# Seven block products for the output projection of one more token tile, with the summed weights made in DRAM

## The chip, the cores and the metric

One Trainium2 chip, one core. The time is the device time of one execution in microseconds; the figure shown for a kernel is the median of its runs.

## The reference

One hybrid encoder block over 2048 tokens of width 1024, in float32. Cut to what matters:

```python
h = rmsnorm(x, w_norm_pre)
q_a, k_a, v_a, z_a, q_r, f_r, i_r, z_r = split(h @ w_in)      # 3328 columns
o_a = sliding_window_sink_attention(rope(q_a), rope(k_a), v_a, sinks) * silu(z_a)
o_r = rmsnorm(hgrn2_chunkwise(q_r, f_r, i_r, lb), hgrn_norm) * silu(z_r)
y = concatenate([o_a, o_r]) @ w_out                            # (2048, 1024) @ (1024, 1024)
out = x + rmsnorm(y, w_norm_post)
```

## The kernel before

The tokens go in four tiles of 512 (TILES, t = 0 to 3). In each tile the tensor engine (PE) first forms 26 column blocks of the input projection (w = 0 to 25: key, value, four queries, four gates, then for each of four recurrent heads forget gate, query, value, gate), 24 matmuls of 128x512 each: eight blocks of the inner dimension, times three for a float32 product made of halves (high x high, low x high, high x low; `products`). Then comes the output projection. Attention and the recurrence of the same tile run between these matmuls, at places that `between` gives (w, m: weight tile and matmul within it): scores of pair q at w = SCORES0 + 2q (8, 10, 12, 14), m = 4; the turn of the previous pair's probabilities right behind; the weighing of the values (`weigh`) at m = 20 of the same weight tile.

Tiles 0 and 1 (t < FAST = 2) use `out_plain`: 8 blocks k x 4 token blocks x 2 column halves x 3 = 192 matmuls of 128x512. Tiles 2 and 3 use `out_fast`, a seven-product scheme after Strassen and Winograd on 2 x 2 blocks: UNITS lists 56 products of three matmuls, 168 in all, over 14 weight tiles (FAST_ROWS). Eight of these (T1 to T4, two weight tiles each, T_TILES = 8) are sums of quarters of the output weights; the sums of the activations are made on the vector engine (DVE) in `sum_head`.

Each weight tile (128x1024, 512 KB) is needed as a rounded high part and a low remainder. For i < FRESH = 40 (i counts weight tiles over all token tiles: all 34 of tile 0 and the first six of tile 1) SP loads the raw weights (`load_raw`, L450) into four slots; the scalar engine (ACT) rounds (`split_hi`, L926) some three steps before use, DVE subtracts (`split_lo`, L1261), and SP saves both parts to DRAM (`save_split`, L458; rows `kept`). A rounding into one of the four split slots waits for the save of the tile that was there (`wait_saved`). From i = 40 on SP loads both parts back (`load_split`, L469).

The summed weights of `out_fast` are made by DVE (`sum_weights`): SP loads four quarters, DVE makes four sums (L1458), ACT rounds (`sums_high`, L1012), DVE subtracts (L1463), SP saves. Half of it happens at the end of tile 1, the other half in steps 5 to 8 of tile 2 (SUMS_AT = 5).

Every engine's order is written by hand, as a loop over t and steps s; step s runs beside weight tile w = s or so, and an engine works strictly in order. In ACT's step: the swap for the rope of the block before (L1066, s - 1 in ROPE_TILES = 0, 2, 3, 4, 5), then gates (`gate_first` L930 to L932, `gate_second` L941, from s = 7), sums_high, splits, softmax (`exp_scores`), `place_values`, and the placement of the values of attention (L1154, s = 2 to 5). In DVE's step: the rope turn (`rope_turn`, L1323 to L1330, s - 2 in ROPE_TILES, so the last in s = 7), gate scaling (L1337), softmax_first, gate_first, sum_weights, splits. PE's first scores wait for the last rope turn (`roped`). GpSimd does small float32 work only; its first wait in tile 0 that is not set-up is in step 18 (L1713, L1697). SP runs a few weight tiles ahead of PE.

The entry: the first two column blocks of tile 0 (K_TILE, V_TILE) follow the order ENTRY, blocks k = 0 to 3 of the first, then of the second, then pairs, as x and weights arrive in parts; FILL puts extra small matmuls in (L877). The sum over x squared (`sum_x`, L589) stands in weight tile 2 at m = 16.

## Time and profile before

| | |
|---|---|
| median of 3 runs | 865.8 us (865.51 to 867.25) |
| the profiled execution | 867.9 us, its span 866.1 us, granted clock 0.997 |
| PE | 853.7 us busy, 99% of the span, 4430 matmuls |
| DVE | 631.8 us, 73% |
| ACT | 518.7 us, 60% |
| GpSimd | 114.6 us, 13% |
| DMA | 211.20 MB, mean 244 GB/s; queue q1 64.5% of 16 engines |

A busy PE counts from the start of a matmul to its modelled end; matmuls overlap (0.39 us each at a start every 0.23), so the starts in the timeline tell more than the busy time.

### The profile page before, as it was taken

To read this page: it belongs to the slowest core of one execution; us is meant where nothing else is said; L and a number is where in the kernel's file an instruction comes from. 1 tells how busy PE (TensorE), PEld (TensorE's weight loads), DVE (VectorE), ACT (ScalarE), POOL (GpSimd) and SP (SyncE) were. 2 spreads that over 40 slices of the span, in tenths; PEclk is the share of its full clock that TensorE was granted. 3 is DMA by queue.
4 is the path that set the end of the run, shared out by engine and by line. 5 is a ranking of instruction groups with operands and counts; after the bars stand their busy time and mean duration, and the time that the engine had idled before them with its cause. 6 is when DMAs were issued, how large, how long until landed. Compare 5 with 4: busy or idle time off the path is not lost.

```text
span 866.1 us, 12450 instructions
## 1 busy us (share of the span) xinstructions
PE 853.7 (99%) x4430; PEld 701.8 (81%) x4430; DVE 631.8 (73%) x1125; ACT 518.7 (60%) x1033; POOL 114.6 (13%) x84
## 2 busy tenths in 40 slices
PE   7999999999999999999999999999999999999997
PEld 6887788888888778888888877888888887888885
DVE  5768878684556799767846789887775368888846
ACT  6756556664556558577436655866753755576544
POOL 0000003521200000433020000144300000004220
PEclk9999999999999999999999999999999999999999
DMA  8587554847987636553899794445699674434586
GB/s 314 182 329 250 219 208 160 314 146 277 418 336 258 228 136 255 182 185 137 312 386 365 257 351 158 159 146 217 226 375 390 236 281 146 146 147 152 193 323 254
DMA packets 59981, 211.20 MB, mean 244 GB/s; under 512 B 6672, under 2 KB 6928, under 8 KB 59920
## 3 DMA queue, kind: packets, MB, share of 16 engines
q1 hardware_dynamic: 57904, 205.56, 64.5%
q10 hardware_dynamic: 2016, 4.85, 1.4%
q8 instruction: 35, 0.57, 0.3%
q14 instruction: 26, 0.21, 0.1%
HBM read 157.95 MB, written 52.43 MB: 243 GB/s over the span
## 4 chain that ended last, share of the span: by engine, by line
PE 80%; DVE 11%; ACT 5%; issue 3%; DMA 1%; SPq 0%; DVEq 0%
PE bank L596 52%; PE bank L605 5%; PE turn_b L852 3%; PE score_b L852 3%; PE bank L852 3%; PE turn_b L605 3%; PE score_b L605 3%; DVE kv_tok L1383 2%; PE turn_b L653 2%; PE score_b L629 2%; PE turn_b L706 1%; PE bank L687 1%; PE turn_b L709 1%; PE bank L697 1%; ACT probs_t L953 1%
## 5 line engine op out<-in xcount | busy, mean ns | idle before, releaser
L596 PE MATMUL bank<-h_hi,w_lo 128*128 128x512 f32 x832 | 327.9, 394 | 0.0
L596 PE MATMUL bank<-h_hi,w_hi 128*128 128x512 f32 x832 | 325.1, 392 | 2.1 <-ACT h_hi L980 2.1
L596 PE MATMUL bank<-h_lo,w_hi 128*128 128x512 f32 x832 | 326.5, 392 | 0.0
L596 PEld LDWEIGHTS bank<-h_hi,w_hi 128*128 128x128 f32 x832 | 156.8, 188 | 34.8 <-ACT h_hi L980 2.6
L596 PEld LDWEIGHTS bank<-h_lo,w_hi 128*128 128x128 f32 x832 | 156.7, 188 | 34.8 <-issue 3.3
L596 PEld LDWEIGHTS bank<-h_hi,w_lo 128*128 128x128 f32 x832 | 156.6, 188 | 33.3 <-issue 0.2
L1713 POOL TENSOR_TENSOR mix_lo<-v_r,mix_hi 128x512 fp32r<-128x512 f32 x16 | 21.2, 1324 | 542.3 <-ACT v_r L1140 542.3
L1261 DVE TENSOR_TENSOR w_lo<-w_raw,w_hi 128x1024 fp32r<-128x1024 f32 x37 | 45.9, 1247 | 35.9 <-ACT w_hi L926 35.4
L1383 DVE STREAM_TRANSPOSE kv_tok<-k_mid 32x128 f32<-32x128 f32 x192 | 58.1, 303 | 2.8
L926 ACT ACTIVATE w_hi<-w_raw 128x1024 fp32r<-128x1024 f32 x38 | 39.7, 1050 | 25.0 <-issue 10.2
L1697 POOL TENSOR_TENSOR x_acc<-x_acc,x_sq 128x512 f32<-128x512 f32 x21 | 32.7, 1559 | 70.0 <-ACT x_sq L976 70.0
L930 ACT ACTIVATE g_a<-g_b 128x512 f32<-128x512 f32 x30 | 18.9, 630 | 38.2 <-DVE g_b L1337 38.2
L941 ACT ACTIVATE g_a<-g_a 128x512 f32<-128x512 f32 x32 | 20.2, 632 | 34.3 <-DVE g_a L1341 34.3
L1066 ACT ACTIVATE f_b<-bank 32x512 f32<-32x512 f32 x48 | 28.3, 589 | 16.5 <-PE bank L596 10.6
L962 ACT ACTIVATE kv_tok<-f_d 32x128 f32<-32x128 f32 x96 | 29.5, 307 | 10.0 <-DVE f_d L1577 9.0
L1341 DVE SCALAR_TENSOR_TENSOR g_a<-g_b,g_a 128x512 f32<-128x512 f32 x30 | 21.6, 722 | 18.3 <-ACT g_a L932 18.3
L962 ACT ACTIVATE probs<-f_d 32x128 f32<-32x128 f32 x96 | 29.5, 307 | 1.2
L1634 DVE TENSOR_TENSOR_SCAN f_c<-reset,f_b 128x512 f32<-128x512 f32 x16 | 19.6, 1224 | 11.3 <-ACT f_b L1123 11.3
L1251 DVE SCALAR_TENSOR_TENSOR h_lo<-x_in,vec,h_hi 128x512 fp32r<-128x512 f32 x32 | 23.3, 773 | 4.8 <-ACT h_hi L980 4.7
L1476 DVE SCALAR_TENSOR_TENSOR q_gate<-q_gate,y_stats,x_in 128x512 f32<-128x512 f32 x28 | 23.1, 873 | 4.5 <-DMA x_in<-in_x_rows 3.6
L605 PE MATMUL bank<-w_hi,mix_lo 128*128 128x512 f32 x64 | 25.3, 395 | 0.0
L605 PE MATMUL bank<-w_hi,mix_hi 128*128 128x512 f32 x64 | 24.9, 390 | 0.0
(280 smaller groups left out, 1549.8 us busy)
## 6 DMA issues: line engine op xcount, KB each, us to landing
w_hi<-kept_hi SPq DMA_DIRECT2D x108, 512.0 KB, 3.7
w_lo<-kept_lo SPq DMA_DIRECT2D x108, 512.0 KB, 4.8
w_raw<-in_weights SPq DMA_DIRECT2D x46, 512.0 KB, 5.9
kept_hi<-w_hi SPq DMA_DIRECT2D x34, 512.0 KB, 6.2
kept_lo<-w_lo SPq DMA_DIRECT2D x34, 512.0 KB, 7.1
x_in<-in_x_rows SPq DMA_DIRECT2D x8, 1024.0 KB, 8.0
x_in<-in_x SPq DMA_DIRECT2D x15, 512.0 KB, 6.7
kept_lo<-w_raw SPq DMA_DIRECT2D x8, 512.0 KB, 6.9
```

What stands on the lines that cost most here:

```text
L596: mm = pe.matmul(acc(w)[:, :], stationary[:, s, k, :], moving[:, k, :], start=(m == 0), stop=(m == 3 * KT - 1), skip_group_check=True)
L605: mm = pe.matmul(y_bank[half][b][:, :], mix[:, k, b * P:(b + 1) * P], weight[:, SPLIT_SLOT[index(t, w)], (k % 2) * 4:(k % 2) * 4 + 4, :].r ...
L852: mm = pe.matmul(into, mix, weight, start=w in (P1A, P7A, P2A, P4A) and k == 0 and part == 0, stop=k == KT // 2 - 1 and part == 2, skip_gr ...
L926: act.activation(w_hi[:, SPLIT_SLOT[i], :, :], w_raw[:, i % RAW_SLOTS, :, :], ACT.Copy).then_inc(hi_split.sem, 1)
L962: copy = act.activation(square(v_tok(t, h), j, i), square(f_d[:, :], i, j), ACT.Copy)
L1066: copy = act.activation(dst[32 * b:32 * b + 32, :], acc(s - 1)[32 * (b ^ 1):32 * (b ^ 1) + 32, :], ACT.Copy)
L1251: dve.scalar_tensor_tensor(h_lo[:, k, :], x_in[:, k, :], w_pre[:, k:k + 1], h_hi[:, k, :], ALU.mult, ALU.subtract).then_inc(h_lo_done.sem, 1)
L1261: dve.tensor_tensor(w_lo[:, s, :, :], w_raw[:, i % RAW_SLOTS, :, :], w_hi[:, s, :, :], ALU.subtract).then_inc(lo_split.sem, 1)
L1341: dve.scalar_tensor_tensor(g_a[:, :], g_b[:, :], 0.0, gate_log(t, i), ALU.min, ALU.subtract).then_inc(gate_arg.sem, 1)
L1383: last = dve.transpose(square(kv_tok[:, 0, :], j, i), square(k_mid[:, :], i, j))
L1476: dve.scalar_tensor_tensor(y, y, y_scale[:, b:b + 1], x_in[:, 2 * b + half, :], ALU.mult, ALU.add).then_inc(finished.sem, 1)
L1697: pool.tensor_tensor(x_acc[:, :], x_acc[:, :], x_sq[:, :], ALU.add).then_inc(x_added.sem, 1)
```

## The change

FAST goes from 2 to 1: tile 1 too uses `out_fast`. The summed weights are no longer made by DVE but in a DRAM tensor `t_rows`: GpSimd issues, in tile 0 as soon as remainder 6 is made, two copies of 1 MB, two accumulating DMAs, then copy, accumulation, copy, accumulation, each waiting for the one before; T1 = B11 + B12, T3 = B22 + B12, T2 = T3 + B11, T4 = T2 + B21. The signs differ from before, so `sum_head` and `post` change signs. SP loads the eight sums (512 KB each): 0 and 1 at (0, OUT0), 2 and 3 at (1, 0), 4 to 7 at (1, 7) of its order; ACT rounds and DVE subtracts them in steps 3 (two), 4 (two), 5 (two), 6 and 7 (one each) of tile 1; SP saves them between its weight tiles 8 and 17. Buffers are those of the probabilities, a spare of the raw area, the raw slots, and the mix tiles.

The entry goes by blocks of two, V's first half is loaded ahead of x's second pair, the vector load stands behind x's first block, a fourth weight tile is split before the loop, the two loads of `squares` move behind ACT's squares of x and their wait from `sum_x` and DVE to the turn of the values; `sum_x` stands at m = 20 in tile 0; one filler fewer.

```diff
+LATE = 6
...
-FAST = 2
+FAST = 1
...
-SPLIT_SLOT += [w % 4 for w in range(WT)] + [(WT + w) % 4 for w in range(FAST_WT)] * (TILES - FAST)
...
+SPLIT_SLOT += [w % 4 for w in range(FAST_WT)] * (TILES - FAST)
...
-SUMS_IN = (FAST - 1, H0 + 8), (FAST, 5)
-SUMS_OUT = ((FAST, 0, 0), (FAST, 1, 2)), ((FAST, H0, 0), (FAST, H0 + 2, 2))
-SUMS_AT = 5
+SUMS_IN = {(FAST - 1, OUT0): (0, 1), (FAST, 0): (2, 3), (FAST, LATE + 1): (4, 5, 6, 7)}
+SUMS_SPLIT = {3: (0, 1), 4: (2, 3), 5: (4, 5), 6: (6,), 7: (7,)}
+SUMS_OUT = {8: 2, 9: 3, 11: 0, 12: 1, 13: 4, 14: 5, 15: 6, 17: 7}
...
-DVE_LOW = range(3, FRESH)
+DVE_LOW = range(4, FRESH)
...
-ENTRY = [(w, k - lag, part) for first, last in ((0, 4), (4, 6), (6, 8)) for w in (K_TILE, V_TILE)
+ENTRY = [(w, k - lag, part) for first, last in ((0, 2), (2, 4), (4, 6), (6, 8)) for w in (K_TILE, V_TILE)
...
-FILL = {1: 1, 2: 2}
+FILL = {1: 1, 2: 1}
...
-        t_hi = [t_more[:, 0, :, :], t_probs[:, 1, :, :], t_more[:, 1, :, :], t_probs[:, 0, :, :]], \
-               [mix[:, 2 * i:2 * i + 2, :] for mix in (mix_hi, mix_lo) for i in range(2)]
+        t_in = [area[:, i, :, :] for area, n in ((t_more, 2), (t_probs, 2), (w_raw, RAW_SLOTS)) for i in range(n)]
+        t_hi = [mix[:, 2 * i:2 * i + 2, :] for i in (2, 3, 1, 0) for mix in (mix_hi, mix_lo)]
...
-                    sp.wait_ge(t_saved, 16 * 2 * T_TILES)
+                    sp.wait_ge(t_saved, 32 * (T_TILES - 2))
+                    sp.wait_ge(probs_saved, 64)
                 for part, rows in ((w_hi, kept[0]), (w_lo, kept[1])):
                     sp.dma_start(part[:, slot, :, :].bitcast(FP32),
                                  rows[row * P:(row + 1) * P, :].rearrange("p (k m) -> p k m", k=KT)).then_inc(w_ready[slot], 16)
 
-            def load_sums(j):
-
-                if j == 0:
-                    sp.wait_ge(lo_split.sem, lo_split.after(0, 0) + FRESH - 1)
-                else:
-                    sp.wait_ge(t_saved, 16 * T_TILES)
-                for r, w in enumerate((B11, B21, B12, B22)):
-                    sp.dma_start(w_raw[:, r, :, :], weights[(w + j) * P:(w + j + 1) * P, :].rearrange("p (k m) -> p k m", k=KT)).then_inc(t_raw, 16)
-
-            def save_sums(j, first):
-
-                sp.wait_ge(t_high, 4 * j + first + 2)
-                sp.wait_ge(t_low, 4 * j + first + 2)
-                for r, w in ((0, T1), (2, T3)) if first == 0 else ((3, T2), (1, T4)):
-                    rows = slice((w + j) * P, (w + j + 1) * P)
-                    sp.dma_start(kept[0][rows, :].rearrange("p (k m) -> p k m", k=2), t_hi[j][r].bitcast(FP32)).then_inc(t_saved, 16)
-                    sp.dma_start(kept[1][rows, :].rearrange("p (k m) -> p k m", k=KT), w_raw[:, r, :, :]).then_inc(t_saved, 16)
+            def load_sum(k):
+
+                if k == 0:
+                    sp.wait_ge(t_made, 64)
+                if k == 2:
+                    sp.wait_ge(weighed.sem, weighed.after(FAST - 1, PAIRS - 1))
+                    sp.wait_ge(head_mixed.sem, head_mixed.after(FAST - 1, HEADS - 1))
+                if k >= 4:
+                    sp.wait_ge(lo_split.sem, lo_split.after(0, 0) + FRESH - RAW_SLOTS + k - 4)
+                sp.dma_start(t_in[k], t_rows[k * P:(k + 1) * P, :].rearrange("p (k m) -> p k m", k=KT)).then_inc(t_loaded[k], 16)
+
+            def save_sum(k):
+
+                sp.wait_ge(t_low, k + 1)
+                rows, saved = slice((WT + k) * P, (WT + k + 1) * P), probs_saved if k in (2, 3) else t_saved
+                sp.dma_start(kept[0][rows, :].rearrange("p (k m) -> p k m", k=2), t_hi[k].bitcast(FP32)).then_inc(saved, 16)
+                sp.dma_start(kept[1][rows, :].rearrange("p (k m) -> p k m", k=KT), t_in[k]).then_inc(saved, 16)
 
...
-            sp.dma_start(vec[:, :], vectors).then_inc(vec_loaded, 16)
...
             sp.dma_start(x_in[:, 0, :], x[0:P, 0:N]).then_inc(x_head, 16)
+            sp.dma_start(vec[:, :], vectors).then_inc(vec_loaded, 16)
             load_half(K_TILE, 0)
             sp.dma_start(x_in[:, 1, :], x[0:P, N:2 * N]).then_inc(x_quarter[0], 16)
+            load_half(V_TILE, 0)
             load_first_x(2)
-            load_half(V_TILE, 0)
             load_half(K_TILE, 1)
             load_first_x(4)
             load_half(V_TILE, 1)
...
+                    for k in SUMS_IN.get((t, w), ()):
+                        load_sum(k)
                     if i >= FRESH:
                         load_split(t, w)
+                    if t == FAST and w in SUMS_OUT:
+                        save_sum(SUMS_OUT[w])
...
-                if w == XSUM and m == (0 if t else 16):
-                    pe.wait_ge(stored[1], 32)
+                if w == XSUM and m == (0 if t else 20):
                     sum_x(t)
                 if w == V_TURN and m == 4 and t < DVE_TURN:
+                    pe.wait_ge(stored[1], 32)
                     turn_values(t)
                 if m == 4 and not odd:
...
-            for i in range(2):
-                act.dma_start(sq_in[:, i, :], squares[:, i * P:(i + 1) * P]).then_inc(stored[1], 16)
...
-            def sums_high(k):
-
-                act.wait_ge(t_sum, k + 1)
-                if k == 4:
-                    act.wait_ge(t_saved, 16 * T_TILES)
-                r = (0, 2, 3, 1)[k % 4]
-                act.activation(t_hi[k // 4][r], w_raw[:, r, :, :].rearrange("p k m -> p (k m)").rearrange("p (k n) -> p k n", k=2), ACT.Copy).then_inc(t_high, 1)
+            def sum_high(k):
+
+                act.wait_ge(t_loaded[k], 16)
+                act.activation(t_hi[k], t_in[k].rearrange("p k m -> p (k m)").rearrange("p (k n) -> p k n", k=2), ACT.Copy).then_inc(t_high, 1)
 
...
             for k in range(1, KT):
                 act.wait_ge(x_quarter[k // 2], 16)
                 round_h(0, k)
+                if k == 1:
+                    first_hi(V_TILE, 0)
                 if k == 3:
-                    first_hi(V_TILE, 0)
                     first_hi(K_TILE, 1)
                 if k == 5:
                     first_hi(V_TILE, 1)
-            split_hi(2)
+            for i in (2, 3):
+                split_hi(i)
             for k in range(KT):
                 act.activation(q_gate[:, k, :], x_in[:, k, :], ACT.Square).then_inc(x_squared.sem, 1)
+            for i in range(2):
+                act.dma_start(sq_in[:, i, :], squares[:, i * P:(i + 1) * P]).then_inc(stored[1], 16)
...
                             act.wait_ge(head_mixed.sem, head_mixed.after(t, head))
+                            if t == FAST and head == 0:
+                                act.wait_ge(t_saved, 32 * (T_TILES - 2))
...
-                    if t == FAST and s in (SUMS_AT + 1, SUMS_AT + 2):
-                        for k in range(2):
-                            sums_high(4 + 2 * (s - SUMS_AT - 1) + k)
+                    for k in SUMS_SPLIT.get(s, ()) if t == FAST else ():
+                        sum_high(k)
...
                             act.wait_ge(o_done.sem, o_done.after(t, head))
+                            if t == FAST and head == 0:
+                                act.wait_ge(probs_saved, 64)
                             act.activation(o_sq_hi, out_b, ACT.Square)
...
-                        for k in range(4) if t == FAST - 1 else ():
-                            sums_high(k)
...
                 dve.wait_ge(s_low.sem, s_low.after(t, h - 1))
-                dve.tensor_tensor(s_tmp[:, S2, :], h_mix[:, 2 * P:], s3[:, h, :], ALU.subtract).then_inc(s_step, 1)
-                dve.tensor_tensor(s_tmp[:, S1, :], h_mix[:, 2 * P:], a21[:, h, :], ALU.add)
+                dve.scalar_tensor_tensor(s_tmp[:, S2, :], h_mix[:, 2 * P:], -1.0, s3[:, h, :], ALU.mult, ALU.subtract).then_inc(s_step, 1)
+                dve.tensor_tensor(s_tmp[:, S1, :], h_mix[:, 2 * P:], a21[:, h, :], ALU.subtract)
                 dve.wait_ge(s_step, (t - FAST) * HEADS + h + 1)
-                dve.tensor_tensor(s_tmp[:, S4, :], h_mix[:, 0:2 * P], s_tmp[:, S2, :], ALU.subtract).then_inc(s_made.sem, 1)
-
-            def sum_weights(j, part):
-
-                raw = lambda r: w_raw[:, r, :, :]
-                if part < 2:
-                    dve.wait_ge(t_raw, 64 * (j + 1))
-                    for k, dst, a, b in ((0, 0, 2, 0), (1, 2, 3, 2)) if part == 0 else ((2, 3, 3, 0), (3, 1, 1, 3)):
-                        if k:
-                            dve.wait_ge(t_sum, 4 * j + k)
-                        dve.tensor_tensor(raw(dst), raw(a), raw(b), ALU.subtract).then_inc(t_sum, 1)
+                dve.scalar_tensor_tensor(s_tmp[:, S4, :], h_mix[:, 0:2 * P], -1.0, s_tmp[:, S2, :], ALU.mult, ALU.subtract).then_inc(s_made.sem, 1)
+
+            def sum_low(k):
+
+                dve.wait_ge(t_high, k + 1)
+                dve.tensor_tensor(t_in[k], t_in[k], t_hi[k].rearrange("p k n -> p (k n)").rearrange("p (k m) -> p k m", m=P), ALU.subtract).then_inc(t_low, 1)
...
-                    if t == FAST and 0 <= s - SUMS_AT < 4:
-                        sum_weights(1, s - SUMS_AT)
+                    for k in SUMS_SPLIT.get(s, ()) if t == FAST else ():
+                        sum_low(k)
...
-            pool.wait_ge(lo_split.sem, lo_split.after(0, 2))
+            pool.wait_ge(lo_split.sem, lo_split.after(0, 6))
+
+            def sum_start(dst, src):
+                pool.dma_start(t_rows[dst * 2 * P:(dst + 1) * 2 * P, :], src).then_inc(t_base, 16)
+
+            def sum_add(dst, src):
+                pool.dma_start(t_rows[dst * 2 * P:(dst + 1) * 2 * P, :], src, accum_op=ALU.add, max_dma_last_dim=4 * KT * P).then_inc(t_made, 16)
+
+            def block_rows(w):
+                return weights[w * P:(w + 2) * P, :]
+
+            sum_start(0, block_rows(B11))
+            sum_start(1, block_rows(B22))
+            pool.wait_ge(t_base, 32)
+            sum_add(0, block_rows(B12))
+            sum_add(1, block_rows(B12))
+            pool.wait_ge(t_made, 32)
+            sum_start(2, t_rows[2 * P:4 * P, :])
+            pool.wait_ge(t_base, 48)
+            sum_add(2, block_rows(B11))
+            pool.wait_ge(t_made, 48)
+            sum_start(3, t_rows[4 * P:6 * P, :])
+            pool.wait_ge(t_base, 64)
+            sum_add(3, block_rows(B21))
...
+    t_rows = nc.dram_tensor("t_rows", (T_TILES * P, KT * P), FP32, kind="Internal").ap()
```

## Rows read from the trace of the kernel before

**Rows 1.** Stretches: us; busy of PE, PEld, DVE, ACT, POOL; clock; DMA share; GB/s

```profile
229.40:442.95 213.55, 213.55 (x1100) 176.11 (x1099) 159.35 (x288) 132.39 (x284) 33.23 (x24) 1.00 0.65 239
...
442.95:652.30 209.35, 208.82 (x1075) 171.43 (x1074) 161.79 (x301) 130.71 (x277) 33.44 (x22) 1.00 0.70 261
```

**Rows 2.** Timeline of PE, end of tile 0: start us, us, what

```profile
229.17 0.39 PE L605 MATMUL bank<-w_lo,mix_hi 128*128 128x512 f32 x1
229.40 0.39 PE L596 MATMUL bank<-h_hi,w_hi 128*128 128x512 f32 x1
```

**Rows 3.** Timeline of PE, tile 2, state products; in brackets idle time and releaser

```profile
588.42 1.13 PE L697 MATMUL bank<-kv_tok 128*128 128x128 f32 x8 [0.22 <-DVE a_t L1355]
```

**Rows 4.** Instructions on w_raw in tile 2, durations ns min/median/max, first and last start

```profile
L1012 ACT ACTIVATE mix_hi<-w_raw x2: 1043/1053/1063, 478.9 to 486.8; 128x1024 fp32r<-128x1024 f32 x2
...
L1463 DVE TENSOR_TENSOR w_raw<-w_raw,mix_hi x2: 1219/1219/1219, 486.7 to 495.4; 128x1024 f32<-128x1024 f32 x2
```

**Rows 5.** Timeline of tile 2, fourth gate on DVE and first weighing on PE

```profile
502.23 0.69 DVE L1337 TENSOR_TENSOR g_b<-bank,x_scale 128x512 f32<-128x512 f32 x1
...
506.02 1.08 PE L653 MATMUL turn_b<-probs_t,v_win 128*64 128x256 f32 x8
```

**Rows 6.** Timeline of ACT, steps 3 to 7 of tile 1; step 5 of tile 2

```profile
254.19 2.39 ACT L1066 ACTIVATE f_d<-bank 32x512 f32<-32x512 f32 x4
...
265.31 2.39 ACT L1066 ACTIVATE f_b<-bank 32x512 f32<-32x512 f32 x4
...
270.38 0.63 ACT L930 ACTIVATE g_a<-g_b 128x512 f32<-128x512 f32 x1 [1.49 <-DVE g_b L1337]
...
471.03 2.39 ACT L1066 ACTIVATE f_d<-bank 32x512 f32<-32x512 f32 x4 [1.46 <-PE bank L596]
```

**Rows 7.** Timeline of DVE, end of the last rope turn in tile 1

```profile
269.06 0.69 DVE L1330 TENSOR_TENSOR q_gate<-f_a,f_b 128x512 f32<-128x512 f32 x1
```

**Rows 8.** Timeline of PE, first scores and first weighing of tile 1

```profile
274.37 1.16 PE L629 MATMUL score_b<-k_t,q_gate 64*128 64x128 f32 x16
...
292.02 1.08 PE L653 MATMUL turn_b<-probs_t,v_win 128*64 128x256 f32 x8
```

**Rows 9.** Busy time by stretch, columns as in rows 1

```profile
35.00:130.00 95.00, 95.00 (x570) 76.08 (x569) 72.85 (x112) 55.35 (x85) 0.06 (x1) 1.00 0.72 257
...
206.00:245.00 39.00, 39.00 (x173) 32.30 (x173) 20.41 (x24) 16.53 (x35) 5.75 (x4) 1.00 1.02 414
```

**Rows 10.** Timeline of ACT and DVE, late weight splits around the start of tile 1

```profile
228.32 1.06 ACT L926 ACTIVATE w_hi<-w_raw 128x1024 fp32r<-128x1024 f32 x1 [2.70 <-DMA kept_lo<-w_lo]
...
237.72 2.35 DVE L1261 TENSOR_TENSOR w_lo<-w_raw,w_hi 128x1024 fp32r<-128x1024 f32 x2
```

**Rows 11.** Timeline of GpSimd (POOL) and of SP's DMA issues (SPq) in tile 0

```profile
129.94 1.30 POOL L1713 TENSOR_TENSOR mix_lo<-v_r,mix_hi 128x512 fp32r<-128x512 f32 x1 [127.12 <-ACT v_r L1140]
...
34.90 0.33 SPq L450 DMA_DIRECT2D w_raw<-in_weights  x1
...
150.39 0.33 SPq L450 DMA_DIRECT2D w_raw<-in_weights  x1
```

**Rows 12.** Timeline of PE in the entry

```profile
8.80 0.50 PE L596 MATMUL bank<-h_hi,w_hi 128*128 128x512 f32 x1 [1.55 <-ACT h_hi L980]
...
10.81 0.79 PE L596 MATMUL bank<-h_hi,w_hi 128*128 128x512 f32 x1 [0.60 <-ACT h_hi L980]
...
14.33 0.62 PE L596 MATMUL bank<-h_hi,w_hi 128*128 128x512 f32 x2
...
26.14 1.02 PE L589 MATMUL turn_b<-x_acc,ones_r 128*128 128x512 f32 x2
```

**Rows 13.** Timeline of ACT and DVE in the entry

```profile
8.03 0.72 ACT L980 ACTIVATE h_hi<-x_in,vec 128x512 fp32r<-128x512 f32 x1 [2.39 <-DMA x_in<-in_x]
...
23.10 0.69 DVE L1297 TENSOR_TENSOR x_acc<-q_gate 128x512 f32<-128x512 f32 x1
```

More of the change, by code:

```diff
@@ L187, in after, with hybrid_block @@
         return self.per_tile + (sum(self.sizes[:tile]) if tile >= 0 else tile * self.per_tile) + i + 1
-def hybrid_block(nc, x, x_rows, weights, cos, sin, vectors, w_post, squares, out, kept):
+def hybrid_block(nc, x, x_rows, weights, cos, sin, vectors, w_post, squares, out, kept, t_rows):
     ctx = ExitStack()
@@ L550, in _ @@
                         load_tables(t + 1)
-                    if (t, w) in SUMS_IN:
-                        load_sums(SUMS_IN.index((t, w)))
-                    for j in range(2):
-                        for first in (0, 2):
-                            if (t, w, first) in SUMS_OUT[j]:
-                                save_sums(j, first)
                     if w == 1 and t > FAST:
@@ L1277, in _ @@
                     first_lo(K_TILE, 0)
+                if k == 1:
+                    first_lo(V_TILE, 0)
                 if k == 3:
-                    first_lo(V_TILE, 0)
                     first_lo(K_TILE, 1)
@@ L1417, in softmax_first @@
                 dve.wait_ge(turned.sem, turned.after(t, q - 1))
+                if t == FAST and q == 0:
+                    dve.wait_ge(probs_saved, 64)
                 if t == 0 and q == 0:
@@ L1657, in _ @@
                         dve.tensor_scalar(y_bias[:, :], y_sq[:, 0:4], 1.0 / D_MODEL, EPS, ALU.mult, ALU.add).then_inc(y_biased.sem, 1)
-                        for part in range(4) if t == FAST - 1 else ():
-                            sum_weights(0, part)
                 if t >= FAST:
```

36 lines of the change are left out of this document (17 added, 19 removed).

## The prediction

> **What bounds the kernel now.** I read the busy time of each stretch first, cut at the first matmul of each tile. In tile 1 the tensor engine (PE) is busy for all of its 213.55 us at full clock, in tile 2 for 208.82 of 209.35 [rows 1]. Next the timeline of PE: consecutive 128x512 matmuls start every 0.227 us and nothing separates the last of the output projection from the first of the next tile [rows 2]. So a matmul that is not issued is worth 0.227 us, wherever the other engines keep up. After the entry PE's waits are small ones only, such as 0.22 us in front of a state product of tile 2 [rows 3]. That they are few doesn't mean there is slack; how much there is has to be read, place by place, from when the vector engine (DVE) and the scalar engine (ACT) deliver. Tile 2 already runs the seven-product form that tile 1 is to get: it is 4.2 us shorter than tile 1, not the 5.44 that its 24 missing matmuls are worth (24 x 0.227).
>
> **Tile 1's projection.** 192 matmuls become 168: -5.44 us. With them come the head sums of the fast form on DVE, so I also give tile 1 the late state products of tile 2 (the one at 588.42 starts 0.60 after its predecessor where 0.227 is the rule, and there are two such places [rows 3]): +0.7.
>
> **The sums leave DVE.** Eight subtractions of 1.22 us are gone (four at the end of tile 1, four in tile 2's steps 5 and 6), while eight ACT roundings (1.05 us, so about 1.0 each back to back) and eight DVE remainders (1.22) stay [rows 4], now all in tile 1's steps 3 to 7. In tile 2 they vanish. There the weighing of the first pair, at 506.02 [rows 5], starts 0.54 after the matmul before it, on ACT's copy of the turned probabilities, 0.3 late: -0.3.
>
> **What they meet in tile 1.** This is the term that decides. ACT begins step 3 of tile 1 at 254.19 and then works without a pause: four swaps of 2.4 us for the rope, three value placements of 1.27; its last swap starts at 265.31 and the first gate only at 270.38 [rows 6]. DVE ends the last rope turn at 269.7 [rows 7], and PE needs it for the first scores at 274.37 [rows 8]: slack 4.7 us. In program order six roundings now stand ahead of that last swap (two in each of steps 3, 4 and 5): 6 x 1.02 = 6.1, so the swap starts at 271.3 and ends at 273.7. The seventh follows, to 274.75. DVE takes the remainder of sum 6 (its step 6) ahead of the last rope turn (its step 7), so it waits for that rounding: 274.75 + 1.22 = 276.0, and the turn takes 2.0: 278.0. The scores wait from 274.4 to 278.0: 3.6 us. It goes on. The gate of step 7 starts at 278.0, its ACT part 278.7 to 282, the eighth rounding and remainder end at 284.2, and then DVE owes the next gate and the softmax. Adding the durations of the unchanged rows one after another, the normalized probabilities of the first pair are there at 293.1, where PE (3.6 late) turns them at 291.3: 1.8 more. The fourth gate's input is scaled by DVE at 295.45 to 296.1, ACT needs 1.9 for its first part and 1.0 for the copy: the weighing, at 292.02 now [rows 8], starts at 299.15. In all 7.1 us late. By then DVE waits for PE again, so it grows no further. Tile 2 checks the method: there the fourth gate is scaled at 502.23 and the weighing follows at 506.02 [rows 5], the same 3.8 us as 295.45 to 299.15. From both sides: nothing, if ACT were 7 us ahead of where these rows have it, and 9 if every link costs a semaphore more. I take **+7.1**. The longest of these idle stretches (3.6 us) could lower PE's clock; but the matmuls behind it are followed by waits of 1.8 and 1.7 on ACT and DVE, which take up slow matmuls, so nothing is added.
>
> **The megabyte in front of tile 1.** The loads of sums 2 and 3 are put behind the save of i = 30, at about 208.5. From 206 to 245 the DMA engines are full (share 1.02, 414 GB/s) [rows 9], and ACT's roundings of the late weights wait for the saves (228.32) [rows 10]: each megabyte ahead of them costs 1.05/0.414 = 2.5 us, on a chain that through DVE (remainders 237.72 to 240.1 [rows 10], for a tile that PE opens at 240.7) reaches the 254.19 above. Between 0 and 2.5, as these bytes may find a hole in the pacing; I take the middle, **+1.2**. The other loads of sums: two at 150.4 (SP's 26th weight load [rows 11]) where the channel is not full, and four at about 255, wanted at 268. Both hidden; if late, the ACT chain above moves by as much.
>
> **GpSimd's DMAs.** Four copies and four accumulating ones of 1 MB in DRAM, in six rounds that wait for each other. They start when remainder 6 is done (SP's load of i = 10 waits for the same count, 34.90) and must end before GpSimd's first work of its own, 129.94, which queues behind them, and before SP's wait at 150.39 [rows 11], behind which the weight loads queue. In those 95 us the DMA share is 0.72 [rows 9]: 27 us free, against 8 x 1.05 MB, 20 us at 414 GB/s, and perhaps 10 more for the second read of an accumulation. Per round 16 us are to be had. No accumulating DMA and no GpSimd-issued one is in this trace; a 512 KB save lands in 5 to 7 us. Bounds: 0, and some 5 us if the weights' saves are slowed enough for their splits to come late. I take 0, as there are 16 us for what the nearest rows do in 7. The Trainium skill ("DMA: Bandwidth & Descriptors", section Anatomy of one DMA) puts a GpSimd-issued transfer at 2.0 us plus bytes over 436 GB/s; by it the six rounds would be an estimated 29 us or so, and the sum the same. Against the change speaks "SBUF - State Buffer" of the same skill, section Two separate sides: GpSimd can't write its descriptors while VectorE holds the shared port in a 2-port mode. By it the six issues would each be put off by at most an instruction or two, and no row here shows it.
>
> **The entry.** Now PE works at half clock (0.43 us for a matmul) until 14.33, idles 1.55 ahead of 8.80 and 0.60 ahead of 10.81, for x [rows 12]. The new order fills that stretch: K's and V's first two blocks (12 matmuls) need only x's first two and V's first half, which moves ahead of the next x load; and the small-row loads of the squares leave the start. I expect x's second block at 7.3 (8.03 now [rows 13]), V's remainder at 9.4, and so PE without a gap from 8.1; if the clock rises as long after that as it now does after 10.81 (3.5 us), it is full at 11.7. Matmuls done by 14.33: 3 + 7 at 0.43 and 11.6 at 0.227, 21.6 against 14.2 now: -1.7 us. Later blocks follow: x's third pair is rounded by 14.0, wanted at 15. Bounds: -2.3 and -0.5. Above -1.7 stands the sum over x: it is read four matmuls later in its tile (0.9 us), but ACT and DVE first split a fourth tile (1.06 and 1.22 [rows 4, 10]). The sum was ready at 23.8 and used at 26.14 [rows 12, 13]; now 24.2 against 24.9, hidden by 0.6 us.
>
> **The sum.** -5.44 + 0.7 - 0.3 + 7.1 + 1.2 - 1.7 = +1.6 us. The profiled execution took 867.9 (span 866.1), 2.1 above the median 865.8; it would take 869.5, and the median **867.4**. Its own range, by the bounds: 864.5 to 870.
>
> **Rivals.** (A) *The sums are hidden*: no stall in tile 1, the megabyte costs nothing. -5.44 + 0.7 - 0.3 - 1.7 = -6.7: 859.1. For it: PE waits nowhere now, and tile 2 bears the same sums at a cost of 0.3. Against: tile 2's ACT has pauses of 1.5 to 1.8 us per step there, tile 1's has none [rows 6]. 0.20. (B) *Half of it*: ACT's chain in tile 1 is some 3 us shorter than I have it, since the roundings overlap their neighbours and the loads come well; stall 3.5 in place of 7.1, DMA 0: about 862.6. 0.13. (C) *Slower, by the full channel*: the whole megabyte delays the late splits (+2.5 in place of 1.2), and PE stands already at tile 1's third weight tile, whose remainder is ready at 238.9 for 240.7; it decides as soon as the delay passes 1.8 us, and what GpSimd's 8 MB leave behind adds up to 5: 869 to 874. For it, 414 GB/s without a break over 39 us [rows 9]. 0.17. (D) *It doesn't do what it says*: the accumulating DMAs outlast 129.94, and ACT's squares of x wait for GpSimd, then PE: each microsecond over 95 counts once, 875 for 8. 0.05. My forecast keeps 0.45.
>
> **Chances.** A difference of 0.2% (1.7 us) is about what a measurement of this kernel can tell from none. Faster than 864.1: A, B: 0.33. Within: most of my forecast, 0.32. Slower than 867.5: C, D and the upper part of the forecast, 0.35. The range for 8 in 10 cuts half of A and the top of C and D: 859.5 to 870.5.
>
> **What would show it.** PE's waits in the new profile: the scores of tile 1 on DVE's last rope turn (3.6), turn and weighing of its first pair (1.8, 1.7). ACT's chain from step 3 to the first gate of tile 1 without idle, some 22 us long. Tile 1's length near 217 if I am right, near 209 under A; tile 2's near 209. The late splits at 228.3 shifted by up to 2.5 (megabyte). PE continuous from about 8.1 and full clock from about 11.7 (entry). GpSimd's last addition landing well before 129. Wrong would I be if tile 1's ACT begins step 3 much before 254.2 less the entry's gain.

## The result, and the profile after

| | before | after |
|---|---|---|
| median (6 runs each, side by side) | 865.71 us (865.29 to 867.25) | 870.46 us (869.33 to 872.40) |
| the profiled execution | 867.9, span 866.1 | 870.67, span 868.9 |

The ratio is 1.0057 [1.0046, 1.0068]: slower by 4.75 us. 867.4 was predicted, with 859.5 to 870.5 as the range.

The page after, its first part: PE has 26 matmuls fewer and 3 us less to do, and the span is longer.

```profile
span 868.9 us, 12454 instructions
PE 850.7 (98%) x4404; PEld 697.7 (80%) x4404; DVE 634.0 (73%) x1141; ACT 524.9 (60%) x1041; POOL 119.8 (14%) x89
```

The windows of after, cut at the first matmul of tiles 1, 2 and 3, as in [rows 1], and a third stretch around the start of tile 1, as in [rows 9]:

```profile
core 0: us, PE busy (x) PEld busy (x) DVE busy (x) ACT busy (x) POOL busy (x), PEclk, DMA share, GB/s
227.56:446.09 218.53, 211.30 (x1075) 172.79 (x1075) 169.88 (x309) 143.03 (x297) 35.84 (x23) 0.99 0.77 283
446.09:655.08 208.99, 208.62 (x1076) 171.58 (x1074) 153.22 (x295) 126.86 (x272) 30.10 (x19) 1.00 0.65 234
206.00:245.00 39.00, 37.59 (x165) 30.44 (x164) 19.84 (x24) 15.98 (x34) 5.74 (x4) 1.00 1.02 416
```

Tile 1 was 213.55 us long and is 218.53, with 5.44 us of matmuls taken out of it. With those and the 0.7 for state products it would be 208.8, about what tile 2 is. So 9.7 us of waits and slow matmuls have come into this one tile. Tile 2 is 0.4 shorter, tile 3 is unchanged (213.8 both). PE's waits in after, grouped by what ended them (us in total, times, longest):

```profile
PE score_b L630 <- DVE q_gate L1330: 2.8, 1, 2.8
PE bank L597 <- DMA w_lo<-kept_lo: 1.7, 1, 1.7
PE turn_b L654 <- ACT probs_t L1075: 1.3, 1, 1.3
PE turn_b L585 <- DVE w_lo L1260: 0.9, 1, 0.9
PE bank L698 <- DVE a_t L1355: 0.7, 4, 0.2
PE bank L597 <- DVE w_lo L1260: 0.6, 1, 0.6
```

The same waits in PE's timeline (start, duration; idle time before it and its releaser in brackets):

```profile
227.56 0.50 PE L597 MATMUL bank<-h_hi,w_hi 128*128 128x512 f32 x1 [0.56 <-DVE w_lo L1260]
...
238.35 0.39 PE L597 MATMUL bank<-h_lo,w_hi 128*128 128x512 f32 x1
239.59 0.50 PE L585 MATMUL turn_b<-mix_hi,ones_r 128*128 128x512 f32 x1 [0.86 <-DVE w_lo L1260]
...
267.19 0.39 PE L597 MATMUL bank<-h_lo,w_hi 128*128 128x512 f32 x1
269.31 0.50 PE L597 MATMUL bank<-h_hi,w_hi 128*128 128x512 f32 x1 [1.73 <-DMA w_lo<-kept_lo]
...
278.71 1.57 PE L630 MATMUL score_b<-k_t,q_gate 64*128 64x128 f32 x16 [2.76 <-DVE q_gate L1330]
...
280.80 0.63 PE L597 MATMUL bank<-h_lo,w_hi 128*128 128x512 f32 x1
281.23 0.63 PE L597 MATMUL bank<-h_hi,w_hi 128*128 128x512 f32 x1
...
299.75 1.08 PE L654 MATMUL turn_b<-probs_t,v_win 128*64 128x256 f32 x8 [1.27 <-ACT probs_t L1075]
```

The idle time in brackets counts from the modelled end of the matmul before (0.39), where the next could have started after 0.227; so I take starts. 239.59 (the sum over x, in front of the third weight tile, whose remainder it waits for) comes 1.0 late, 269.31 comes 1.9 late and the scores 2.9: 5.8 us. Counted from the tile's first matmul, the scores stood at 44.97 [rows 1, 8] and stand at 51.15, 6.2 later. Behind them PE runs at half clock for a while (280.80 and 281.23, 0.43 apart), some 1.7 us, the turn of the probabilities comes 0.4 late, and the weighing waits 1.3 more: it stood at 62.62 and stands at 72.19, 9.6 later, which is the excess of the whole tile.

What stands behind the scores, in ACT's timeline of after:

```profile
254.75 2.40 ACT L1066 ACTIVATE f_d<-bank 32x512 f32<-32x512 f32 x4
...
271.99 2.40 ACT L1066 ACTIVATE f_b<-bank 32x512 f32<-32x512 f32 x4
274.41 1.06 ACT L1008 ACTIVATE mix_hi<-w_raw 128x1024 fp32r<-128x1024 f32 x1
...
279.29 0.63 ACT L929 ACTIVATE g_a<-g_b 128x512 f32<-128x512 f32 x1 [2.77 <-DVE g_b L1337]
```

and in DVE's:

```profile
275.51 1.22 DVE L1455 TENSOR_TENSOR w_raw<-w_raw,mix_hi 128x1024 f32<-128x1024 f32 x1 [1.46 <-ACT mix_hi L1008]
...
277.97 0.69 DVE L1330 TENSOR_TENSOR q_gate<-f_a,f_b 128x512 f32<-128x512 f32 x1
...
295.97 0.69 DVE L1337 TENSOR_TENSOR g_b<-bank,x_scale 128x512 f32<-128x512 f32 x1
```

This is the forecast chain link by link: ACT works through 21 us without idle, its last swap comes at 271.99 (265.31 before [rows 6]); DVE waits for the seventh rounding before the last rope turn; the turn ends at 278.7 and PE starts its scores then.

### The profile page after: what moved, and what is told of

Same layout as the page of the kernel before. It is cut to its first block, busy times and chain, and to the rows that moved or that the text cites. A ratio compares the mean times of both kernels' runs of the same rounds, so it can differ in the third digit from the quotient of the medians.

```text
span 868.9 us, 12454 instructions
## 1 busy us (share of the span) xinstructions
PE 850.7 (98%) x4404; PEld 697.7 (80%) x4404; DVE 634.0 (73%) x1141; ACT 524.9 (60%) x1041; POOL 119.8 (14%) x89
## 3 DMA queue, kind: packets, MB, share of 16 engines
q0 software_dynamic: 1216, 8.39, 3.7%
## 4 chain that ended last, share of the span: by engine, by line
PE 57%; DVE 20%; ACT 11%; issue 6%; DMA 4%; SPq 1%; POOL 0%; DVEq 0%; ACTq 0%
PE bank L597 38%; PE turn_b L853 4%; PE score_b L853 4%; PE bank L853 4%; DVE kv_tok L1383 4%; DMA kept_lo<-w_lo 3%; ACT probs_t L952 1%; PE score_b L630 1%; PE turn_b L654 1%; DVE q_gate L1472 1%; DMA w_raw<-in_weights 1%; DVE f_c L1630 1%; PE turn_b L707 1%; DVE s_stats L1430 1%; ACT probs L961 1%
## 5 line engine op out<-in xcount | busy, mean ns | idle before, releaser
L929 ACT ACTIVATE g_a<-g_b 128x512 f32<-128x512 f32 x29 | 18.3, 630 | 40.5 <-DVE g_b L1337 40.5
L1066 ACT ACTIVATE f_b<-bank 32x512 f32<-32x512 f32 x48 | 28.3, 590 | 13.9 <-PE bank L597 13.4
L1337 DVE TENSOR_TENSOR g_b<-bank,x_scale 128x512 f32<-128x512 f32 x32 | 21.9, 684 | 3.8 <-PE bank L597 3.1
L1157 ACT ACTIVATE v_win<-g_a 32x128 f32<-32x128 f32 x48 | 14.8, 308 | 14.2 <-DVE g_a L1547 13.5
## 6 DMA issues: line engine op xcount, KB each, us to landing
t_rows<-in_weights POOLq DMA_DIRECT2D x4, 1024.0 KB, 13.4
```

The source lines that it names most:

```text
L1066: copy = act.activation(dst[32 * b:32 * b + 32, :], acc(s - 1)[32 * (b ^ 1):32 * (b ^ 1) + 32, :], ACT.Copy)
L1337: dve.tensor_tensor(g_b[:, :], acc(w)[:, :], x_scale[:, :], ALU.mult).then_inc(tile_read.sem, 1)
```

## The experiments

Each kernel was timed in five rounds beside the kernel before (865.7 to 866.7 in these groups). In the edits, `-` lines are those of after where the kernel is built from after, and of before where it is built from before. Positions are starts in the profiled execution; "first scores" are those of tile 0. A column of waits is the list as above. The medians of before in the five groups differ by 1.0 us among themselves, so a difference between medians of two groups is sure to about 1 us only. Where it matters I give two more: that of the ratios, and that of the profiled executions from the first scores to the end, which is free of the entry (810.2 to 810.5 us in before, 815.7 in after).

**1. The kernel before once more**, unchanged.

> The kernel before once more, unchanged, for a second profile. The profiled execution of before stood 2.2 us above its own median, that of after at its median, so the two profiles differ by 2.8 us and the medians by 4.75. Theory: the entry of before varies between executions, by when PE's clock rises; this profile then has a span of about 864 and the clock full well before 14.3 us, the rest of the kernel as in the first profile. Rival: the difference is spread over the kernel, or is noise of one execution; then this profile shows no earlier clock.

865.96 us, ratio 1.0002 [0.9991, 1.0013]. The profiled execution spans 865.4 us, not the 864 expected. PE's timeline in its entry:

```profile
7.85 0.39 PE L596 MATMUL bank<-h_hi,w_lo 128*128 128x512 f32 x1
8.07 0.40 PE L596 MATMUL bank<-h_lo,w_hi 128*128 128x512 f32 x1
...
10.48 0.79 PE L596 MATMUL bank<-h_hi,w_hi 128*128 128x512 f32 x1 [1.56 <-ACT h_hi L980]
...
13.63 0.41 PE L596 MATMUL bank<-h_lo,w_hi 128*128 128x512 f32 x1
```

PE already runs at 2.4 GHz (some 0.23 from start to start) around 8, falls to half, and is at full speed from 13.6. The first profile of before has the same pattern a little later:

```profile
9.14 0.40 PE L596 MATMUL bank<-h_hi,w_lo 128*128 128x512 f32 x1
9.38 0.40 PE L596 MATMUL bank<-h_lo,w_hi 128*128 128x512 f32 x1
```

0.24 apart, then half speed from 10.81 to 14.33 [rows 12]. So the entry of one program differs from one execution to the next, here by 0.4 us. How much in all, the profiled executions tell together:

| profiled execution | its time | first scores | difference |
|---|---|---|---|
| before | 867.90 | 57.50 | 810.4 |
| before, again | 867.24 | 57.06 | 810.2 |
| accum_alone (below) | 866.17 | 56.02 | 810.2 |
| entry_only (below) | 865.45 | 54.96 | 810.5 |

Four executions whose tiles 1 to 3 are alike differ by 2.5 us, and nearly all of it lies ahead of the first scores. The median of before, 866.0 in this group, puts its usual first scores at about 55.7; this is an inference from these four and the median. The ten profiled executions of kernels with the new entry have them between 54.35 and 55.19.

**2. The new entry alone**, in the kernel before.

```diff
-ENTRY = [... for first, last in ((0, 4), (4, 6), (6, 8)) ...
+ENTRY = [... for first, last in ((0, 2), (2, 4), (4, 6), (6, 8)) ...
-FILL = {1: 1, 2: 2}
+FILL = {1: 1, 2: 1}
```

and all that the change does to the order of the first loads and splits.

> Before with the new entry alone (blocks of two, the moved loads and waits, a fourth tile split early). Theory: against typical executions of before the entry gives only 0.5 to 1 us (median 864.7 to 865.2), since PE's clock often rises early in them anyway. Rival, as forecast: 1.7 to 2.5 us (863.2 to 864).

865.40 us, 0.9991 [0.9981, 1.0000], 0.6 below before in the same group, at the edge of what can be told from nothing (864.7 to 865.2 was expected). In its PE timeline the block from 7.33 on has no gap, and full speed begins at about 9:

```profile
7.33 0.77 PE L596 MATMUL bank<-h_hi,w_hi 128*128 128x512 f32 x1
...
8.76 0.42 PE L596 MATMUL bank<-h_hi,w_lo 128*128 128x512 f32 x1
9.02 0.39 PE L596 MATMUL bank<-h_lo,w_hi 128*128 128x512 f32 x1
```

So the order does what it is meant to do, and the first scores are 2.5 us earlier than in the before profile, but that one was a late execution: against the usual one the gain is 0.6 by the medians and 0.7 by the first scores.

**3. After, with the entry of before.**

```diff
-ENTRY = [... for first, last in ((0, 2), (2, 4), (4, 6), (6, 8)) ...
+ENTRY = [... for first, last in ((0, 4), (4, 6), (6, 8)) ...
```

> After with the entry of before. Theory: entry and tile 1 are additive, so it is slower than after by what entry_only gains (0.5 to 1 by my theory: 871 to 871.5) and all waits of PE in tile 1 (0.7, 1.0, 1.9, 2.8, 1.3) are still there. Rival: the entry's gain is given back ahead of tile 1, where PE now waits for late splits; then old_entry takes as long as after, with smaller waits at 226 and 239.

870.78 us, 1.0049 [1.0034, 1.0065]: 0.3 above after by the medians, but not by the ratios (1.0057 for after). 871 to 871.5 was expected. Tile 1 has its waits still, 3.5 us at the scores among them, and is as long as in after (218.5). So the loss doesn't come from the new entry. That the entry gains anything isn't shown from this side.

**4. The megabyte of sums 2 and 3 six weight tiles later.**

```diff
-SUMS_IN = {..., (FAST, 0): (2, 3), ...
+SUMS_IN = {..., (FAST, LATE): (2, 3), ...
```

> After, with the loads of sums 2 and 3 moved from (1, 0) to (1, 6) of SP's order, out of the stretch in which the DMA engines are full. Theory: the megabyte costs 2.5 to 3 us: ACT begins step 3 of tile 1 near 252.3 instead of 254.75, the waits ahead of tile 1 (0.6) and of the sum over x (0.9) go, the median falls to 867.5 to 868. Rival (my forecast's middle value): 1.2 us, to 869.3. If the DMAs of GpSimd are what made the saves late: no change.

867.93 us, 1.0019 [1.0010, 1.0028], as expected (867.5 to 868): 2.5 below after by the medians, 3.3 by the ratios, 2.4 from the first scores on. The rows of after on which this bears, SP's issue of the two loads and ACT's roundings of the late weights behind them:

```profile
205.41 1.42 SPq L484 DMA_DIRECT2D t_probs<-t_rows  x2
```

```profile
225.18 1.06 ACT L925 ACTIVATE w_hi<-w_raw 128x1024 fp32r<-128x1024 f32 x1 [5.72 <-DMA kept_lo<-w_lo]
228.93 1.06 ACT L925 ACTIVATE w_hi<-w_raw 128x1024 fp32r<-128x1024 f32 x1 [2.69 <-DMA kept_lo<-w_lo]
```

Against the first scores of the same execution the second stands at 173.96; before, it was 228.32 [rows 10], at 170.82: 3.1 later. In mb_late it starts at 226.10, at 171.39. ACT's start of step 3 follows:

```profile
252.14 2.39 ACT L1066 ACTIVATE f_d<-bank 32x512 f32<-32x512 f32 x4
```

at 197.43 after the first scores; 196.69 in before and 199.78 in after. One pair of profiles could be chance. But in the four profiles that have the megabyte early (after, old_entry, split_early, loads_apart) this start stands at 198.9 to 199.8, in the six that have it late at 196.4 to 197.4, and in the four without sums in tile 1 at 195.5 to 196.7: the means of the first two sets are 2.4 apart. The waits of mb_late, where those in front of tile 1 and in front of the sum over x (0.6 and 0.9) are gone:

```profile
PE bank L597 <- DMA w_lo<-kept_lo: 2.1, 1, 2.1
PE score_b L630 <- DVE q_gate L1330: 2.0, 1, 2.0
PE turn_b L654 <- ACT probs_t L1075: 1.3, 1, 1.3
```

Tile 1 is 216.77 long, 1.8 less than in after, and the end of tile 0 is 0.6 shorter. What is left over 208.8 is 8.0, the price of the sums' work on ACT and DVE: from its step 3 (252.14) to the weighing (297.11) it is 44.97 us, as long as in after.

**5. The sums split elsewhere**: four in step 2, and one each in steps 5, 7, 8 and 9. Only the one of step 5 is left between ACT's start of step 3 and the last rope turn. Here and in 6, 7, placed, 11 and 12 the roundings and remainders of the sums also stand behind the splits of weights in their step and no longer ahead of them.

```diff
-SUMS_SPLIT = {3: (0, 1), 4: (2, 3), 5: (4, 5), 6: (6,), 7: (7,)}
+SUMS_SPLIT = {2: (0, 1, 2, 3), 5: (4,), 7: (5,), 8: (6,), 9: (7,)}
```

> After with another placing of the eight roundings and remainders in tile 1, the same work: four in step 2, behind the split there, where ACT idles 3.9 us and then DVE 3.7, one each in steps 5, 7, 8, 9. Theory (the chain of roundings ahead of the last rope turn is what costs): the waits at the scores (2.8) and the weighing (1.3) and PE's slow clock behind them (1.2 and some in the scores) go, 5 to 6 us, to about 865; the waits for late splits (0.6, 0.9) and for weight tile 7 (1.7) stay. Rival (the tile is held by DMA traffic as a whole): these waits move elsewhere, 869 to 870.

865.78 us, 0.9997 [0.9988, 1.0006]: 4.7 below after by the medians, 5.2 by the ratios, 4.8 from the first scores on. The wait at the scores is gone. A wait of 2.1 for the load of weight tile 7 and one of 1.4 at the weighing remain. With the same work in other steps, the slower result has become no change.

**6. Both, 4 and 5.**

> split_early and mb_late together. Theory: 1.6 us less than split_early, since PE's waits ahead of tile 1 and of the sum over x go too, to 863 to 863.5; the wait for weight tile 7 behind the four loads of sums stays with about 2. Rival: both remove the same waits, then as split_early.

864.13 us, 0.9974 [0.9963, 0.9986], where 863 to 863.5 was expected. The two gains don't add: 2.4 and 4.8 from the first scores on, and 5.7 together. The wait for weight tile 7's load is 2.3 now, and PE runs at 0.43 per matmul from 267.8 to 270.8 behind it. In after this wait cost nothing of its own, since PE would have waited for the rope turn ten microseconds later anyway.

**7. The loads of sums 4 to 7 one by one**, each beside a weight tile of its own from the eighth on, in place of all four (2 MB) ahead of the loads of weight tiles 7 and 8.

```diff
-SUMS_IN = {..., (FAST, LATE + 1): (4, 5, 6, 7)}
+SUMS_IN = {..., (FAST, LATE + 2): (4,), (FAST, LATE + 3): (5,), (FAST, LATE + 4): (6,), (FAST, LATE + 5): (7,)}
```

> both_fixes with the loads of sums 4 to 7 one by one (at weight tiles 8 to 11 of SP's order) instead of four in front of weight tile 7's load. Theory: the wait for weight tile 7 goes, 2 us less than both_fixes: 861 to 861.5, the 24 missing matmuls and the entry in full. If 7 waits anyway, as both_fixes.

865.88 us, 0.9992 [0.9982, 1.0001]: 861 to 861.5 was expected, a miss. Weight tile 7 waits no more: the scores stand at 44.98 in the tile, as in before, and at 49.23 in both_fixes. And yet the weighing comes at 67.0 (62.6 in before, 67.3 in both_fixes): ACT and DVE set it, with the roundings and remainders of sums 5 to 7 between the gates. None of these three roundings waits for its load; the one of sum 4 does, 2.5 us, in front of the last swap. Ahead of the weighing PE waits 1.6 us in front of the turn of the probabilities, runs at half speed from 288.2 to 291.6, and waits 0.9 more. A wait taken off PE moved to the next link that was as late. Why the median is 1.8 above that of both_fixes, where the two profiled executions take the same time (span 862.7 and 862.6), is open.

**8. GpSimd's eight DMAs alone**, in the kernel before, from remainder 6 of tile 0 on, their results unused.

```diff
+            sum_start(0, block_rows(B11))
+            sum_start(1, block_rows(B22))
+            pool.wait_ge(t_base, 32)
+            sum_add(0, block_rows(B12))
...
+            sum_add(3, block_rows(B21))
```

> Before with GpSimd's eight DMAs of 1 MB in tile 0 added, their results unused. Theory: the saves and loads of weights land later (6 to 7 us before, 9 to 18 in after while the chain runs), but PE waits for none: 866.0, within 0.4. Rival: each megabyte counts as it does ahead of tile 1, some 2.4 us for each millisecond-free stretch, 868 or more.

866.41 us, 1.0005 [0.9995, 1.0016], against 866.34 for before: no difference, within 1.4 us. From the first scores on it is 810.2 us, as in before. The chain itself in after, from GpSimd's timeline (L1702 are copies, L1705 accumulating DMAs; in brackets how long the queue waited, and for what):

```profile
33.58 1.21 POOL L1702 DMA_DIRECT2D t_rows<-in_weights  x2 [30.75 <-DVE w_lo L1260]
46.75 1.86 POOL L1705 DMA_DIRECT2D t_rows<-in_weights  x2 [11.96 <-DMA t_rows<-in_weights]
68.38 0.52 POOL L1702 DMA_DIRECT2D t_rows<-t_rows  x1 [19.76 <-DMA t_rows<-in_weights]
77.02 0.87 POOL L1705 DMA_DIRECT2D t_rows<-in_weights  x1 [8.13 <-DMA t_rows<-t_rows]
90.24 0.52 POOL L1702 DMA_DIRECT2D t_rows<-t_rows  x1 [12.34 <-DMA t_rows<-in_weights]
99.03 0.88 POOL L1705 DMA_DIRECT2D t_rows<-in_weights  x1 [8.28 <-DMA t_rows<-t_rows]
127.32 1.36 POOL L1730 TENSOR_TENSOR mix_lo<-v_r,mix_hi 128x512 fp32r<-128x512 f32 x1 [27.41 <-ACT v_r L1143]
```

and from the page's list of DMA issues (count, KB each, median us from issue to landing):

```profile
t_rows<-in_weights POOLq DMA_DIRECT2D x4, 1024.0 KB, 13.4
```

Each round takes 8.6 to 21.6 us, the last begins at 99.0 and, at 13.4, ends at about 112: 15 us ahead of GpSimd's first work of its own. The stretch of the DMAs in after, and the same in before (columns as in [rows 1]):

```profile
30.00:120.00 90.00, 90.00 (x523) 72.19 (x522) 74.14 (x114) 54.20 (x82) 5.86 (x8) 1.00 0.97 334
30.00:120.00 90.00, 90.00 (x522) 72.19 (x521) 73.19 (x112) 55.64 (x85) 0.00 (x0) 1.00 0.68 242
```

The DMA engines are full here too (share 0.97; 1.03 from 35 to 115). GpSimd's 8.39 MB take 35.3% of the stretch, 32 us. The saves of the weights land 15.7 and 18.3 us after their issue in the median (high and low part; 5.7 and 6.8 in before), and no wait of PE comes of it. In this stretch ACT waits for no save at all; in front of tile 1, where the share is the same, it idles 2.7 to 5.7 us for them. So a full channel alone cost nothing here. The Trainium skill ("DMA: Bandwidth & Descriptors", section Anatomy of one DMA) has 2.0 us plus bytes over 436 GB/s, an estimated 31 us for the six rounds (12 and, for 8.39 MB, 19). The trace doesn't agree: they took some 79, beside the kernel's own traffic.

**9. and 10. Placement again.** "placed" has spread's loads and puts sums 6 and 7 behind the softmax; "loads_apart" is after with spread's loads alone.

```diff
+SUMS_SPLIT = {2: (0, 1, 2, 3), 5: (4,), 6: (5,), 11: (6,), 12: (7,)}
```

> spread with the last three roundings and remainders at steps 6, 11 and 12 instead of 7, 8 and 9: out of the steps between the first gate and the first weighing, where every remainder (1.2 us) is one link of DVE's and ACT's chain to that weighing. Theory: spread's weighing, 67.0 us after the tile's first matmul (62.6 in before), comes back to 63 to 64, the tile shortens from 213.4 to 209.5 to 210.5, the median by 3 us to 862.5 to 863. Rival: PE's own slow clock ahead of the weighing made spread's loss, independent of the placement; then 865.5 as spread.

> After with the loads of sums 4 to 7 one by one (weight tiles 8 to 11 of SP's order) and nothing else changed. Theory: PE's wait for weight tile 7 (1.7 us) goes, but the wait at the first scores grows by as much, since DVE's last rope turn sets it; time as after, 870 to 870.8. Rival: waits add up; then 868.7.

placed: 867.10 us, 1.0011 [1.0002, 1.0021], where 862.5 to 863 was expected. loads_apart: 875.85 us, 1.0107 [1.0091, 1.0124], where no change was expected. Both missed for one reason. ACT's timeline in loads_apart:

```profile
274.34 1.06 ACT L1008 ACTIVATE mix_lo<-w_raw 128x1024 fp32r<-128x1024 f32 x1 [5.14 <-DMA w_raw<-t_rows]
...
276.70 2.38 ACT L1066 ACTIVATE f_b<-bank 32x512 f32<-32x512 f32 x4
```

A rounding waits 5.14 us for its load, and the last swap of the rope (276.70; 271.99 in after) queues behind it. PE then waits 4.9 and 5.8 us. In placed ACT waits 3.09 and 1.76 for such loads, PE waits 3.6 at the scores, and the matmuls behind run at half speed for some 4 us. A load that is late for work off PE's path is on it as soon as that work stands ahead of the rope on an engine that keeps order. (loads_apart has four executions only, 873.78 to 877.13.)

**11. Four sums in step 2, then one in each of steps 5 to 8**, with the late megabyte and after's block of four loads.

```diff
+SUMS_SPLIT = {2: (0, 1, 2, 3), 5: (4,), 6: (5,), 7: (6,), 8: (7,)}
```

> both_fixes with the single roundings at steps 5, 6, 7, 8 instead of 5, 7, 8, 9; loads as there (all four in front of weight tile 7). Theory: one remainder fewer between the first gate and the first weighing, whose sum with its wait for ACT is some 1.2 to 2 us; the first scores have 4.7 us of slack for the two ahead of them. 862.5 to 863.5 against 864.1. Rival: the wait for weight tile 7 (2.3) and the slow clock behind it set the tile: as both_fixes.

864.34 us, 0.9977 [0.9968, 0.9987]: 862.5 to 863.5 was expected, a miss; it is as both_fixes. Weight tile 7 waits 1.1, the turn of the probabilities 0.7, the weighing 1.3.

**12. Two loads and two**: sums 4 and 5 loaded where all four were, 6 and 7 three and four weight tiles later, split behind the softmax.

```diff
-SUMS_IN = {(FAST - 1, OUT0): (0, 1), (FAST, 0): (2, 3), (FAST, LATE + 1): (4, 5, 6, 7)}
-SUMS_SPLIT = {3: (0, 1), 4: (2, 3), 5: (4, 5), 6: (6,), 7: (7,)}
+SUMS_IN = {(FAST - 1, OUT0): (0, 1), (FAST, LATE): (2, 3), (FAST, LATE + 1): (4, 5), (FAST, LATE + 4): (6,), (FAST, LATE + 5): (7,)}
+SUMS_SPLIT = {2: (0, 1, 2, 3), 5: (4,), 6: (5,), 11: (6,), 12: (7,)}
```

> placed with the loads of sums 4 and 5 again in front of weight tile 7 (6 and 7 as in placed). Theory: placed lost 3.6 us at the first scores because ACT waited 3.1 and 1.8 us for these loads to land; issued some microseconds earlier they are there, PE waits about 1 us for weight tile 7 instead, and 1.4 at the second weighing as in placed: 863.5 to 864.5. Rival: the channel is so full that they land as late: 866 to 867.

862.82 us (862.03 to 863.79), 0.9958 [0.9944, 0.9973] (863.5 to 864.5 was expected): faster than both kernels. It is 7.6 us below after by the medians, 8.6 by the ratios, 7.7 from the first scores on. Tile 1 is 211.53 long. Its waits:

```profile
PE turn_b L654 <- ACT probs_t L952: 1.5, 2, 1.2
PE turn_b L654 <- ACT probs_t L1075: 1.2, 1, 1.2
```

No load and no rope turn holds PE; its longer waits are for the probabilities of the weighings. Tile 1 is still 2.7 us over its 208.8. By the ratio the kernel is 3.6 us faster than before.

## Why the prediction was wrong, step by step

The sign of the sum was right (+1.6), and so was the mechanism of its largest terms; it was 3.1 us too low. Three terms were mis-sized: the megabyte by 1.3 us (+1.2 taken, 2.5 measured), the entry by 1.1 (-1.7 taken, -0.6 measured) and the chain of ACT and DVE by 0.9 (+7.1 taken, 8.0 measured, of which 0.7 is probably scatter). The range "by the bounds", 864.5 to 870, was also narrower than the bounds of its terms: no chain, no megabyte and an entry of -2.3 would give 858.5. Term by term:

- **The matmuls, -5.44**, and **the state products, +0.7**: tile 2, which has both, lasts 208.99, and 213.55 - 5.44 + 0.7 is 208.8. They hold. **Tile 2, -0.3**: it is 0.4 shorter.
- **The chain of ACT and DVE, +7.1**: the mechanism and its length held. From ACT's start of step 3 to the weighing the prediction has 254.19 to 299.15, 44.96 us; after shows 254.75 to 299.75, 45.00. With the megabyte out of the way (mb_late) tile 1's excess is 8.0, and the same stretch 44.97. ACT starts 0.7 us later there than in before, against the first scores; in the five other kernels with the late megabyte the start lies from 0.3 earlier to 0.3 later than in before, so these 0.7 are most likely scatter between executions and no term of their own. The wait at the scores is 2.8 and not 3.6, as PE had already stood 1.7 for a load on the way.
- **The megabyte, +1.2**: mis-sized, 2.5 by mb_late (2.4 to 3.3, by what is compared). Both ends stood in the text, and the middle was taken because the bytes might find a hole. In a stretch with a share of 1.02 [rows 9] there is none, and the arithmetic, 1.05 MB at 414 GB/s, was itself the answer. Rival C had this price; with it C's mechanism came true, PE's wait for the third weight tile's remainder (239.59) included, without what it added for GpSimd. The measured time lies in C's range. Half of it needed slack on the chain, and the ACT row at 228.32 [rows 10] says that there is none: it idles for a save.
- **"The other loads of sums are hidden"** was false: the four at 255 stand ahead of weight tile 7's loads in SP's order, and it waited 1.7. The step read when the sums are wanted, and not what is queued behind their issue. It cost nothing in after only because the rope's wait came behind it, which is luck; both_fixes makes it visible (2.3, and 3 us of half speed behind it), spread takes it away.
- **GpSimd's DMAs, 0**: right (accum_alone), and 15 us were left of the 95. The round of the first two accumulations, 21.6, is above the 16 that the prediction gave to each; the rounds of single copies, 8.6 and 8.8, make up for it. The 20 us of bytes and perhaps 10 for the second read are near the 32 us that the DMA engines spent; the 27 us that it called free were used up, and the saves landed three times as late without PE waiting for one. By the page that it cites its estimate of 29 us should have been 31.
- **The entry, -1.7**: mis-sized, by what it was compared with. Its mechanism is there (no gap from 7.3 on in entry_only, full speed from 9 to 10 where 11.7 was expected), and against the profile of before it gives even 2.5. The working misread that profile twice: PE doesn't run at half speed all the way to 14.33 (the rows at 9.14 and 9.38 are 0.24 apart), and it starts 12 matmuls of 128x512 before 14.33, not 14.2; after starts 25, not 21.6. What failed is the step from there to the median. The profile of before was an execution with a slow entry: its first scores stood 1.8 us behind the usual 55.7, and its time 1.9 above the median. The prediction counted 1.7 us saved from the slow entry, and then subtracted 2.1 more as a constant. By these first scores the constant was, for the most part, the entry itself. For after, profile and median differ by 0.2. Measured alone the entry is worth 0.6 (entry_only), hardly clear of nothing; old_entry shows 0.3 or nothing.
- **The clock adds nothing**: right for after. It fell behind the scores' wait (280.8 to 282.5, 1.2 GHz by the distance of 0.43) and the weighing waits behind it, set by ACT and DVE, so that the slow matmuls cost nothing of their own: the chain from step 3 to the weighing has its forecast length with them. In both_fixes, where nothing later waits for long, they cost: eight matmuls at 0.43 lose 1.6 us.

The sum with these sizes is -5.44 + 0.7 - 0.4 + 8.0 + 2.5 - 0.6 = +4.8; 4.75 was measured. That it fits so closely is partly chance, as none of the last three terms is sure to better than some tenths. Rival A (hidden, 859.1) fell with tile 1's ACT; B with the length of the chain; D with the DMAs' landing.

## What to carry to other kernels

Before a profile's own time is brought to the median, find where it lies apart from other executions of the same kernel; an edit in that place must not be credited with it twice. Where a tuned engine shows no waits, slack has to be read from the order of the engines that feed it: move extra work on them behind the last link that the bottleneck needs soon, and order its loads so that neither they nor what is queued behind them is late. A term between 0 and full price was at full price here where its channel was at a share of 1 and the engine behind it already idled for that channel; at a share of 1 without such an engine (GpSimd's DMAs) it cost nothing.
